# Block-product projections: the rounded block and its low part as one 512-wide operand, halves added on GpSimd

## The reference, cut to what matters

```
proj = hn @ w_in                       # hn: (512, 2048)
q, k, v, z, f_logit = split(proj)      # 16 heads x 128 each for q, k, v, z
o = forgetting_attention(q, k, v, log_sigmoid(f_logit + b_forget))
x + (o * silu(z)) @ w_out
```

## Time and profile before

| | us |
|---|---|
| median of 3 runs (lowest, highest) | 2948.53 (2948.32, 2949.63) |
| the profiled execution, its own time | 2949.23 |
| its span, first to last instruction | 2947.40 |
| mean granted TensorE clock, of full speed | 0.995 |

### The profile page before, as it was taken

The page is one execution under the profiler, slowest core; times in us unless marked ns, Lnnn a source line. Parts: engine busy times, 40 slices in busy tenths (PEclk is TensorE's granted clock), DMA queues, the critical chain, the costliest instruction groups (busy, mean ns, idle before and its releaser), DMA issues. The chain is left out here.

```text
span 2947.4 us, 52822 instructions
## 1 busy us (share of the span) xinstructions
PE 2888.1 (98%) x20478; PEld 2430.1 (82%) x20478; DVE 1539.2 (52%) x2031; ACT 1333.6 (45%) x1858; POOL 1410.3 (48%) x1031
## 2 busy tenths in 40 slices
PE   8999999999999999999999999999999999999998
PEld 6777777777787887778787777887999999999886
DVE  7556655434444117778733335118666666666412
ACT  5434434245565323333434554325555555556422
POOL 1223322433324544667743334544566666666643
PEclk9999999999999999999999999999999999999999
DMA  5111111222212443222242223442232323332433
GB/s 219 60 60 59 52 56 55 90 82 80 78 57 85 165 139 100 97 90 96 86 147 93 91 88 111 162 138 80 97 107 104 110 96 106 104 108 98 161 125 114
DMA packets 98561, 298.17 MB, mean 101 GB/s; under 512 B 10608, under 2 KB 16880, under 8 KB 97408
## 3 DMA queue, kind: packets, MB, share of 16 engines
q1 hardware_dynamic: 71440, 246.12, 24.5%
q10 hardware_dynamic: 26992, 50.22, 5.2%
HBM read 273.45 MB, written 22.84 MB: 101 GB/s over the span
## 5 line engine op out<-in xcount | busy, mean ns | idle before, releaser
L3416 POOL TENSOR_TENSOR w_lo<-raw,w_hi 128x512 fp32r<-128x512 f32 x624 | 844.6, 1376 | 1217.2 <-ACT w_hi L768 1216.1
L338 PE MATMUL ps<-act_hi,w_hi 128*128 128x512 f32 x1232 | 486.4, 395 | 10.8 <-POOL w_lo L3416 5.0
L768 ACT ACTIVATE w_hi<-raw 128x1024 fp32r<-128x1024 f32 x316 | 333.6, 1056 | 357.3 <-PE ps L340 135.3
L339 PE MATMUL ps<-act_hi,w_lo 128*128 128x512 f32 x1232 | 481.0, 390 | 0.0
L340 PE MATMUL ps<-act_lo,w_hi 128*128 128x512 f32 x1232 | 480.9, 390 | 0.0
L2187 POOL TENSOR_TENSOR w_lo<-arena,w_hi 128x512 fp32r<-128x512 f32 x150 | 227.5, 1537 | 183.0 <-ACT w_hi L2110 183.0
L1035 PE MATMUL ps<-act_hi,w_hi 128*128 128x512 f32 x736 | 294.2, 400 | 0.0
L338 PEld LDWEIGHTS ps<-act_hi,w_hi 128*128 128x128 f32 x1232 | 231.9, 188 | 72.7 <-issue 16.1
L1036 PE MATMUL ps<-act_hi,w_lo 128*128 128x512 f32 x736 | 286.9, 390 | 0.0
L1037 PE MATMUL ps<-act_lo,w_hi 128*128 128x512 f32 x736 | 286.7, 390 | 0.0
L2093 PE MATMUL ps<-act_hi,w_hi 128*128 128x256 f32 x960 | 274.2, 286 | 2.1 <-POOL w_lo L2187 2.1
(11 more groups left out here) (501 smaller groups left out, 5895.8 us busy)
## 6 DMA issues: line engine op xcount, KB each, us to landing
raw<-stream SPq DMA_DIRECT2D x378, 512.0 KB, 3.3
arena<-stream SPq DMA_DIRECT2D x64, 512.0 KB, 3.3
residual<-mix ACTq DMA_DIRECT2D x32, 256.0 KB, 2.0
arena<-residual ACTq DMA_DIRECT2D x32, 256.0 KB, 2.7
arena<-x_rows SPq DMA_DIRECT2D x4, 1024.0 KB, 18.3
arena<-x ACTq DMA_DIRECT2D x16, 256.0 KB, 2.7
kept_qk<-mix ACTq DMA_DIRECT2D x16, 256.0 KB, 2.0
arena<-kept_qk ACTq DMA_DIRECT2D x16, 256.0 KB, 3.8
```

Source lines behind the costliest of these rows:

```text
L338: pe.matmul(dst, w_hi[:, slot, j, :], act_hi[:, a, :], start=first, stop=False)
L339: pe.matmul(dst, w_lo[:, slot, j, :], act_hi[:, a, :], start=False, stop=False)
L768: nc.scalar.activation(w_hi[:, s, :, :], src[:, s % 2, :, :], ACT.Copy).then_inc(cast_done, 1)
L3416: last = nc.gpsimd.tensor_tensor(w_lo[:, s, part, :], raw[:, s % 2, part, :], w_hi[:, s, part, :].bitcast(F32), ALU.subtract)
```

## The change

- Rounded operand and low part lie in one tensor (`acts`, and `cells_r` with `mix` and the arena together), so that `w7_both(i, j)` is one operand of two 256-column pieces. For each of the 8 row tiles of a product PE does one 512-wide matmul (w_hi by hi, and by lo, into the left and right half of the bank) and one 256-wide (w_lo by hi, into the left half): 16 matmuls a product instead of 24.
- A bank now holds a sum in two halves. All seven evacuations are 512 wide. GpSimd adds the halves of the four results in 256-wide additions f12, f22, f11, f21 (`w7_fold_out`). For a pair p, f12 stands in GpSimd's program ahead of lo0 of pair p + 1, and f22, f11, f21 between its lo0 and lo3; the last pair's four stand after the loop, ahead of `out3_gpsimd`.
- Waits: x5 also waits for the f22 before it, x2 for the f21; the value transposes wait for f21 (before: c11 and c21), the Silu of the gate for f22 (before: c22), the split of q and k for f21 (before: c21).
- The operand of product 4 moves to another place in `mix`: `fold_round` of 3 now waits for `fold_rest` of 4, and two loads at the end wait for one product more.

```diff
-        act_hi = sb("act_hi", [P, KT, T], F32R)
-        act_lo = sb("act_lo", [P, KT, T], F32R)
+        acts = sb("acts", [P, 2 * KT * T], F32R)
+        act_hi, act_lo = (slots(acts, KT * j, KT).rearrange("p (k t) -> p k t", k=KT) for j in range(2))
...
+        def w7_both(i, j):
+
+            view, hi, lo = w7_places[i]
+            first, second = sorted((hi[j], lo[j]))
+            return view[:, first:second + 1:second - first, :]
...
         def fold_round(act, name, q):
-            if name in "34":
+            if name == "4":
                 act.wait_ge(pe_half, 2 * (N_ODD + 3) + 1)
+            elif name == "3":
+                fold_dve.wait(act, f"l4{q}", 0)
...
-        x1, x5, x2 = (w7_x[:, j, :] for j in range(3))
+        x1, x2, x5 = w7_x[:, 0, :], w7_x[:, 1, :], at_cum
...
-            return ps[:, pp, 0:HT], ps[:, 1 - pp, 0:HT]
+            return ps[:, pp, :], ps[:, 1 - pp, :]
...
-                sp.wait_ge(w7_pe, 7 * last + 4)
+                sp.wait_ge(w7_pe, 7 * last + 5)
...
-            hi, lo = w7_acts[i]
+            halves = dst.rearrange("p (a t) -> p a t", a=2)
             first = i in (0, 1, 5)
             for j in range(HK):
-                pe.matmul(dst, w_hi[:, slot, j, :], hi[:, j, :], start=first and j == 0, stop=False,
+                pe.matmul(halves, w_hi[:, slot, j, :], w7_both(i, j), start=first and j == 0, stop=False,
                           skip_group_check=True)
-                pe.matmul(dst, w_lo[:, slot, j, :], hi[:, j, :], start=False, stop=False, skip_group_check=True)
-                mm = pe.matmul(dst, w_hi[:, slot, j, :], lo[:, j, :], start=False, stop=j == HK - 1,
+                mm = pe.matmul(dst[:, 0:HT], w_lo[:, slot, j, :], w7_hi_of(i, j), start=False, stop=j == HK - 1,
                                skip_group_check=True)
...
             elif name == "x5":
                 act.wait_ge(w7_pe, p * 7 + 2)
+                if not first_pair(u, pp):
+                    w7_fold.wait(act, "f22", p - 1)
...
-                w7_out.mark(nc.vector.tensor_tensor(second[:, 0:HT], d, x2, ALU.add), name)
+                w7_out.mark(add(second, d, x2, ALU.add), name)
...
+        def w7_fold_out(pool, u, pp, name):
...
+            if name == "f12":
+                w7_fold.start(p)
+                w7_out.wait(pool, "c12", p)
+                w7_fold.mark(add(second[:, 0:HT], second[:, 0:HT], second[:, HT:T], ALU.add), name)
+            elif name == "f22":
+                w7_fold.wait(pool, "f12", p)
+                w7_out.wait(pool, "c22", p)
+                w7_fold.mark(add(second[:, HT:T], x5[:, 0:HT], x5[:, HT:T], ALU.add), name)
+            elif name == "f11":
+                w7_out.wait(pool, "c11", p)
+                w7_fold.mark(add(first[:, 0:HT], first[:, 0:HT], first[:, HT:T], ALU.add), name)
+            else:
+                w7_fold.wait(pool, "f11", p)
+                w7_part.wait(pool, "c21", p)
+                w7_fold.mark(add(first[:, HT:T], x2[:, 0:HT], x2[:, HT:T], ALU.add), name)
...
                 for pp in range(2):
+                    later = not first_pair(u, pp)
+                    if later:
+                        w7_fold_out(pool, u, pp - 1, "f12")
                     for i in W7_POOL[first_pair(u, pp):]:
...
                         last.then_inc(w7_lo, 1)
+                        if later and i == 0:
+                            for name in ("f22", "f11", "f21"):
+                                w7_fold_out(pool, u, pp - 1, name)
...
+            for name in ("f12", "f22", "f11", "f21"):
+                w7_fold_out(pool, W7_UNITS - 1, 1, name)
...
-                    w7_out.wait(pe, "c11", at_pair(u, -1))
-                    w7_part.wait(pe, "c21", at_pair(u, -1))
+                    w7_fold.wait(pe, "f21", at_pair(u, -1))
...
-                w7_out.wait(act, "c22", at_pair(u, 1))
+                w7_fold.wait(act, "f22", at_pair(u, 1))
...
-                w7_part.wait(dve, "c21", at_pair(u, 0))
+                w7_fold.wait(dve, "f21", at_pair(u, 0))
```

More of the change, by code:

```diff
@@ L188, in sem @@
             return ctx.enter_context(nc.semaphore(name))
-        act_hi = sb("act_hi", [P, KT, T], F32R)
-        act_lo = sb("act_lo", [P, KT, T], F32R)
-        with nc.sbuf_tensor("mix_r", [P, KT * T], F32R) as rounded:
-            mix_r = rounded
-        mix = sb("mix", [P, KT * T])
+        acts = sb("acts", [P, 2 * KT * T], F32R)
+        act_hi, act_lo = (slots(acts, KT * j, KT).rearrange("p (k t) -> p k t", k=KT) for j in range(2))
+        with nc.sbuf_tensor("cells_r", [P, (KT + 30) * T], F32R) as rounded:
+            cells_r = rounded
+        cells = sb("cells", [P, (KT + 30) * T])
+        mix, mix_r = (slots(view, 0, KT) for view in (cells, cells_r))
+        arena, arena_r = (slots(view, KT, 30) for view in (cells, cells_r))
         raw = sb("raw", [P, 2, HK, P])
@@ L1874, in build_program, with every_half, every, w7_hi_of @@
                  "3": half_k(mix_k[:, low_k, :], 1), "4": half_k(mix_k[:, high_k, :], 0)}
-        s_hi = {"1": eight(arena_r, 26), "2": eight(arena_r, 18), "3": half_k(act_hi[:, low_k, :], 1),
-                "4": half_k(act_lo[:, low_k, :], 1)}
+        s_hi = {"1": eight(arena_r, 26), "2": eight(arena_r, 18), "3": half_k(mix_k_r[:, high_k, :], 0),
+                "4": half_k(act_hi[:, low_k, :], 1)}
         s_lo = {"1": half_k(mix_k_r[:, high_k, :], 1), "2": half_k(mix_k_r[:, low_k, :], 0),
[L1878 to L1885, removed]
+                "3": half_k(mix_k_r[:, low_k, :], 1), "4": half_k(act_lo[:, low_k, :], 1)}
+        def every_half(first, half):
+            return [2 * first + 2 * j + half for j in range(HK)]
+        def every(first):
+            return [2 * first + j for j in range(HK)]
+        act_halves, cell_halves = (view[:, :].rearrange("p (s t) -> p s t", t=HT) for view in (acts, cells_r))
+        w7_places = ((act_halves, every_half(0, 0), every_half(KT, 0)),
+                     (cell_halves, every(KT + 26), every_half(HK, 1)),
+                     (cell_halves, every(KT + 18), every_half(0, 0)),
+                     (act_halves, every_half(0, 1), every_half(KT, 1)),
+                     (cell_halves, every_half(HK, 0), every_half(0, 1)),
+                     (act_halves, every_half(HK, 0), every_half(KT + HK, 0)),
+                     (act_halves, every_half(HK, 1), every_half(KT + HK, 1)))
+        def w7_hi_of(i, j):
+            view, hi, _ = w7_places[i]
+            return view[:, hi[j], :]
+        def w7_both(i, j):
+            view, hi, lo = w7_places[i]
+            first, second = sorted((hi[j], lo[j]))
+            return view[:, first:second + 1:second - first, :]
         fold_sum = Steps(sem("fold_sum"), "s10 s30 s20 s40 s11 s31 s21 s41")
@@ L1942, in build_program @@
         w7_out = Steps(sem("w7_out"), "c12 c22 c11")
+        w7_fold = Steps(sem("w7_fold"), "f12 f22 f11 f21")
         w7_part = Steps(sem("w7_part"), "x1 x5 x2 c21")
@@ L2125, in w7_part_out @@
                 act.wait_ge(w7_pe, p * 7 + 3)
+                if not first_pair(u, pp):
+                    w7_fold.wait(act, "f21", p - 1)
                 w7_part.mark(nc.scalar.activation(x2, b, ACT.Copy), name)
@@ L2134, in w7_sum_out @@
             b, d = w7_banks(pp)
-            second = (at_k_in, at_gate)[pp]
+            first, second = ((at_q_in, at_k_in), (at_v_in, at_gate))[pp]
+            add = nc.vector.tensor_tensor
             if name == "c12":
@@ L2451, in unit @@
                 scaled(u)
-                w7_sum_out(dve, u, 0, "c12")
-                w7_sum_out(dve, u, 0, "c22")
+                for name in ("c12", "c22"):
+                    w7_sum_out(dve, u, 0, name)
                 turned(u)
```

20 lines of the change are left out of this document (10 added, 10 removed).

## The result

The changed kernel takes 2987.3 us (median of 4 runs, 2985.81 to 2989.17) against 2948.43 us (2947.97 to 2949.63) beside it: ratio 1.0131, 95% interval 1.0118 to 1.0143. The prediction was 3004 us in a range of 2957 to 3028: slower as forecast, by 38.9 us where 55.5 were forecast. The profiled execution has a span of 2984.4 us, 37.0 more than before.

What follows compares the result with a forecast made beforehand. The loop through GpSimd, VectorE and ScalarE was taken as the bound, with little slack beside PE. Additions 65.0 less slack 7.0, less 3 at the start, plus 2 at the end gave +57; lowered to 3004 us, range 2957 to 3028.

Steps and rivals of the forecast that it cites:

- the queue loop: Closed loop of GpSimd, VectorE and ScalarE in the forgetting-attention stage, once round per weight pair, nearly as long as PE's work.
- Rival A: PE stays the bound because the loop has over 1.5 us of room beside the additions: 2924 us, chance 0.08.
- PE's saving: Fewer matmuls in the products: 13.8 ns a block, 23.2 us over 1680 blocks, not taken off because PE then waits.
- B: Rival: the additions delay GpSimd but don't hold VectorE, so only f12's delay of lo0 stays: 2961 us, chance 0.17.
- The additions: Four GpSimd additions a pair lengthen the loop by 2.24 us; over 29 pairs 65.0 us.
- Step 1: f12 stands ahead of lo0 in GpSimd's queue, so lo0 is late by 0.71 us a pair.
- Step 2: f22, straight behind lo0, holds the shared port against VectorE's T1: 0.58 us more a pair.
- step 3: f11, waiting for c11 behind T1, holds the port against l1: 0.28 us more a pair.
- step 4: f21 asks inside l1, gets the port at l1's end ahead of T2: 0.67 us more a pair.
- The slack: Room of the loop beside PE's work, about 0.5 us in a 45.6 us unit; 7.0 us off over 14 units.
- Start: Stage's start: h3 waits for l4, so l4 and l3 no longer run at once; about 3 us back (0 to 5).
- End: Stage's end: f21 delays the value transposes and the first output tile's split; +2 us (0 to 3).

Runs made afterwards that it cites:

- the spare additions: Kernel before, plus four 256-wide GpSimd additions a pair in the change's four places, results read by nobody: 2979.81 us, ratio 1.0107.

## Why the prediction held, and where its numbers were off

*The bound.* Right. PE was busy for 98% of the span, and still the queue loop was nearly as long as PE's work, 44.76 us beside 45.62, and the additions made it the bound. Rival A is refuted: PE's saving is off the path. B is refuted by the spare additions and T1's 1.65 us: the port takes 0.91 of the 1.60 us a pair. The outcome lies between B's 2961 and the forecast, and inside the forecast's own 2985 to 3018.

*The additions, 2.24 us a pair forecast, 1.60 measured.* Step 1 was 0.69 for 0.71. Step 2 was 0.42 for 0.58, step 3 0.07 for 0.28, step 4 0.42 for 0.67. The order of the four and what holds what were as written. The error is in the sum of a hold: I let the held instruction run its full 1.23 us once the port was free. But T1 asks at 2417.99, f22 ends at 2418.56, and T1 ends at 2419.64, 1.08 us after. So 0.15 us go off each hold of steps 2, 3 and 4, which is 0.45 of the 0.64 us. f21, held itself, runs 0.60 us past l1 and not 0.67, and f11 asks 0.68 us behind T1's end and not 0.74. Over 29 pairs the 0.64 us are 18.6 us, a little more than the whole excess of the forecast (17).

*The slack, 0.5 us a unit forecast, 0.86 measured*: 5 us more off. I read it from a single wait (x5, 0.75 us) of one unit, and missed that for most of the stage T2 meets lo3 in every second unit, where the room is gone. The sum still takes 0.86, because the change ends this meeting, which the prediction did not say. The unit's sum then closes, 44.76 + 2 x 1.60 = 47.96 us against 48.06, and so does the whole: the +57 of the forecast, less 18.6 and 5, with 1.5 and 1.1 more at start and end and 1.3 before the stage, are 37.3 against the span's 37.0. That it closes so well is in part luck, since the 1.3 differ from trace to trace.

*PE's saving, 23.2 us forecast and not counted.* The two pitches of the earlier trace rows were each taken in long runs of one width. In turn a pair costs 354 ns and not 346.8, and the measured saving was 11.6 us (0.77 us x 15 units). It changed nothing here, but rival A would have ended near 2936 us and not 2924. By the Trainium skill, TensorE: Matmul & The Clock Gate, Back-to-back issue gap, with its fixed 2.5 ns for each matmul, the estimate for a dropped one is 2.5 ns, which is 4.4 under the 6.9 ns measured.

*Start and end.* Start: -3 forecast, -1.5 in the first unit. l4 takes 2.36 us where it took 6.77, and product 1's wait is gone, as written. But T2, now beside l3, takes 3.25 us, and product 2 waits 3.28 us. VectorE and PE by time:

```profile
2052.27 2.36 DVE L1955 TENSOR_TENSOR acts<-cells,acts 128x1024 fp32r<-128x1024 f32 x2
...
2058.24 3.25 DVE L2211 TENSOR_TENSOR raw<-cells,raw 128x1024 f32<-128x1024 f32 x1
```
```profile
2064.98 0.79 PE L2116 MATMUL ps<-cells_r,w_hi 128*128 128x512 f32 x1 [3.28 <-DVE w_lo L2223]
...
2066.43 0.63 PE L2116 MATMUL ps<-cells_r,w_hi 128*128 128x512 f32 x1
...
2067.07 0.63 PE L2116 MATMUL ps<-cells_r,w_hi 128*128 128x512 f32 x1
```

The wait moved more than it went: before has waits of 2.48 and 2.12 us in the first unit, after of 3.28 and 0.95 us. Behind the 3.28 us the blocks come every 0.64 us (2066.43, 2067.07) and not 0.35, at a granted clock of 0.50 (1.2 GHz). In before the matmuls behind the 2.48 us come every 0.21 us and not 0.12 at the same clock, so its price stayed too. Of the 1.5 us gained the cheaper matmuls are 0.8. End: +2 forecast, +3.1 measured, and the clock's 2.4 us were in no term.

*What the profile should have shown.* Waits for l1 and l2, c11 at 0.68, T2 held and additions near 0.74 came as written. T1 was 1.65 for 1.8. PE was busy 96% of the stage and not 91%: its need of 44.85 us in a unit of 48.06 is 93%, since the blocks were longer and the unit shorter than forecast, and the view counts each matmul to a modelled end. A wait of product 4 for lo4 I find only in the first unit (0.95 us).

## What to carry to other kernels

Before moving work onto a half-idle engine, measure the closed loop through its queue: one spare instruction in a planned place, in the old kernel, gives the loop's room, and spares in all the planned places give the price of the port too. Four spare additions here foretold 2.1 of the 2.4 us a unit without building the change. Read the loop over several units: one unit hid that the loop was longer in every second one. And when matmuls are fused, take the pitch of the sequence that will run, not of each width by itself.

## What the runs showed of the hardware that was not expected

- A VectorE instruction held off by GpSimd does not need its full time once the port is free: T1, l1 and T2 (128x1024, two SBUF inputs) end 1.08 us after the GpSimd instruction that held them, where they take 1.23 alone. It shows as a longer instruction and not as idle time. (The Trainium skill, Advanced Engine Details and Errata, GPSIMD Details, has the conflict; T1 at 1.65 us agrees, and these numbers are the trace's.)
- Who asks 0.09 us earlier gets the port for its whole instruction: T2 1.23 or 2.28 us. A kernel can so alternate between two unit lengths, 46.14 and 47.23 us, and the kernel before does so inside its loop (T2 1.23 or 2.31 us) while its units stay at 45.62.
- 512- and 256-wide matmuls in turn take 354.0 ns a pair, eight and eight grouped 349.1 (medians of product 3), and 346.8 by their own pitches. One run or two in the operand makes no difference.
- The granted clock follows waits of a few us in a stage that is otherwise full. Two waits of PE of 1.91 and 2.74 us, with 0.66 us of work between, were followed by a granted clock of 0.50 for 12 matmuls, and one of 2.59 us by some eight. A wait of 1.37 us at the same place, with the additions on VectorE, was not.
